# A two-model transformer kernel: a weight split moved behind the fifth step of the pair attention, early softmax inverses, and ScalarE's selection rows of the second mixer spread over four chunks

## What is computed

```python
def first_block(x, c, ctx, ...):                  # x and ctx: 256 tokens each
    for l in range(2):
        hx, hc = modulate(rms_norm(x, ...)), modulate(rms_norm(ctx, ...))
        qa, ka, va, qb, kb, vb, qc, kc, vc = split(hx @ w_in[l])      # and the same of hc
        oa = softmax attention, 8 heads;  ob = neighbourhood attention, 4 heads
        oc = diff_attend: (softmax(q0 k0) - lam * softmax(q1 k1)) v, 4 heads, then rms_norm
        x = x + gt1_x * (concat(oa, ob, oc) @ w_out[l])
        x = x + gt2_x * conv_ffn(...)             # in layer 0 the same for ctx
def second_block(x, meta_tokens, ...):            # 16 meta tokens + 256 tokens
    for l in range(2):
        h = h + 0.5 * rmsnorm(swiglu(...));  h = h + rmsnorm(token_mixer(...));  h = h + 0.5 * rmsnorm(swiglu(...))
def token_mixer(h, ...):
    fq, fk, fv, ff, gq, gk, gv, ga, gr, g_merge_a, g_merge_b = split(h @ w_in)
    log_f = log_sigmoid(ff + b_f)
    o_fox = fox_attention(fq, fk, fv, log_f)      # s + cum[q] - cum[k], softmax, 8 heads
    o_gla = gla_chunked(gq, gk, gv, log_a)        # exp of differences of cumulated log_a
    return (sigmoid(g_merge_a) * (o_fox @ w_fox_o) + sigmoid(g_merge_b) * (o_gla @ w_gla_o)) @ w_out
```

## Time and profile before

| | us |
|---|---|
| median of 3 runs | 2352.1 |
| lowest and highest | 2344.34 and 2356.29 |
| the profiled execution, device time | 2353.69 |
| its span, first to last instruction | 2351.9 |
| PE busy / DVE / ACT / POOL | 2301.4 / 1561.0 / 1207.0 / 145.0 |
| mean granted TensorE clock, of full | 0.988 |

### The profile page before, as it was taken

One profiled execution on the slowest core, in us unless ns is written; L12 is line 12 of the kernel. 1 busy time (PEld: TensorE's weight loads), 2 busy tenths in 40 slices (PEclk: granted clock), 3 DMA queues, 4 the chain that ended last, 5 costly groups with the idle time before them and its releaser, 6 DMA issues.

```text
span 2351.9 us, 46522 instructions
## 1 busy us (share of the span) xinstructions
PE 2301.4 (98%) x17227; PEld 2102.8 (89%) x17227; DVE 1561.0 (66%) x2770; ACT 1207.0 (51%) x2061; POOL 145.0 (6%) x252
## 2 busy tenths in 40 slices
PE   7999999999999999999999999999999999999998
PEld 5787788888878789999999889999999999899998
DVE  5546678887877458865655745766566557467764
ACT  4647544443237556654445555554454455656553
POOL 1214200000010220000000000000000000000000
PEclk9999999999999899999999999999999999999999
DMA  8750234444645025565555434455545553354654
GB/s 321 242 176 1 66 106 161 146 144 147 197 137 159 32 69 166 181 181 166 181 174 156 126 99 144 144 182 173 172 150 181 171 161 127 99 167 148 204 179 126
DMA packets 101199, 356.42 MB, mean 152 GB/s; under 512 B 11344, under 2 KB 13040, under 8 KB 101072
## 3 DMA queue, kind: packets, MB, share of 16 engines
q1 hardware_dynamic: 86704, 304.45, 40.5%
q0 software_dynamic: 14368, 50.24, 6.6%
HBM read 352.55 MB, written 1.05 MB: 150 GB/s over the span
## 4 chain that ended last, share of the span: by engine, by line
PE 92%; ACT 3%; DVE 3%; issue 1%; DMA 1%; SPq 0%; DVEq 0%; ACTq 0%
PE ps L782 25%; PE ps L784 25%; PE ps L783 25%; PE ps L957 2%; PE ps L973 2%; PE ps L940 2%; PE ps L799 2%; PE ps L803 1%; PE ps L800 1%; DMA ada_raw<-in_w_ada 1%; PE ps L1224 1%; PE ps L870 1%; ACT wh L1358 1%; PE ps L1266 1%; DVE wl L1848 1%
## 5 line engine op out<-in xcount | busy, mean ns | idle before, releaser
L1848 DVE TENSOR_TENSOR wl<-raw,wh 128x1024 fp32r<-128x1024 f32 x574 | 701.5, 1223 | 403.0 <-ACT wh L1358 402.4
L782 PE MATMUL ps<-hH,wh 128*128 128x272 f32 (+2 forms) x2880 | 888.5, 309 | 4.0 <-DVE silu L2548 3.1
L783 PE MATMUL ps<-hL,wh 128*128 128x272 f32 (+2 forms) x2880 | 876.7, 304 | 0.0
L784 PE MATMUL ps<-hH,wl 128*128 128x272 f32 (+2 forms) x2880 | 876.7, 304 | 0.0
L1358 ACT ACTIVATE wh<-raw 128x1024 fp32r<-128x1024 f32 x574 | 602.6, 1052 | 323.4 <-PE ps L784 305.5
L782 PEld LDWEIGHTS ps<-hH,wh 128*128 128x128 f32 x2880 | 545.4, 189 | 33.4 <-issue 4.3
L783 PEld LDWEIGHTS ps<-hL,wh 128*128 128x128 f32 x2880 | 545.3, 189 | 20.4 <-issue 0.2
L784 PEld LDWEIGHTS ps<-hH,wl 128*128 128x128 f32 x2880 | 545.5, 189 | 19.9
L784 PE MATMUL ps<-actH,wl 128*128 128x272 f32 (+2 forms) x1184 | 358.5, 303 | 0.0
L782 PE MATMUL ps<-actH,wh 128*128 128x272 f32 (+2 forms) x1184 | 356.4, 301 | 0.2 <-ACT actH L1518 0.2
L783 PE MATMUL ps<-actL,wh 128*128 128x272 f32 (+2 forms) x1184 | 356.4, 301 | 0.0
(11 more groups left out here) (308 smaller groups left out, 2803.4 us busy)
## 6 DMA issues: line engine op xcount, KB each, us to landing
raw<-in_w_ffn_gu SPq DMA_DIRECT2D x176, 512.0 KB, 3.5
raw<-in_w_mix SPq DMA_DIRECT2D x98, 512.0 KB, 3.5
raw<-in_w_up SPq DMA_DIRECT2D x88, 512.0 KB, 3.5
raw<-in_w_ffn_down SPq DMA_DIRECT2D x64, 512.0 KB, 3.6
ada_rest<-in_w_ada POOLq DMA_DIRECT2D x32, 512.0 KB, 4.8
raw<-in_w_out SPq DMA_DIRECT2D x32, 512.0 KB, 3.5
raw<-in_w_down SPq DMA_DIRECT2D x32, 512.0 KB, 3.5
raw<-in_w_qk SPq DMA_DIRECT2D x26, 512.0 KB, 5.2
```

What stands on the lines that cost most here:

```text
L782: pe.matmul(out, a_h, b_h, start=start, stop=False)
L783: pe.matmul(out, a_h, b_l, start=False, stop=False)
L784: return pe.matmul(out, a_l, b_h, start=False, stop=stop)
L1848: dve.tensor_tensor(wl[:, slot, :], raw[:, slot, :], wh[:, slot, :].bitcast(F32), ALU.subtract).then_inc(l_split, 1)
```

## The change

It has five parts.

1. In the pair attention the transposes of steps 0 and 1 come one position earlier: a new function `turned_at(i)` gives step 0 at i = 2, step 1 at i = 3, none at i = 4, and i-3 from i = 5 on. PE, ACT's copies and DVE's copies follow it.
2. The reciprocals of steps 0 and 1 move out of the loop, to right behind the exponentials of each, beside the values' projection (new function `inverse`).
3. ACT does the exponentials of step 1 ahead of its last copy to `v_tok`, and DVE the copy L2434 ahead of the last `rest_rows` and without a split in front of it.
4. The fifth split of stage `v{l}` (chunk 2 of `out{l}`), ACT's half and DVE's half, moves from the end of the values' stage to the end of i = 5 of the attention's loop. The table load L1436 goes.
5. In the mixers the four `nsel` instructions move from `ci` = 8, where they stood ahead of the edges' exponentials, to `ci` = 11, 12, 13 and 14, one each, behind the exponential of that chunk's level. The wait of the forgetting attention's first scores counts 4 per layer instead of 1.

```diff
+        def turned_at(i):
+
+            return i - 2 if i in (2, 3) else i - 3 if i >= 5 else None
...
@@ PE, pair_attention
-                    if 3 <= i < n + 3:
-                        turn(run[i - 3])
+                    if turned_at(i) is not None and turned_at(i) < n:
+                        turn(run[turned_at(i)])
@@ PE, scores of the forgetting attention
-                        pe.wait_ge(mix_set, l + 1)
+                        pe.wait_ge(mix_set, 4 * (l + 1))
@@ ACT, pair_attention
-                act.preload_act_table_set("natural_log_exp_and_others")
...
-                    if 3 <= i < n + 3:
-                        copy_even(run[i - 3])
+                    if turned_at(i) is not None and turned_at(i) < n:
+                        copy_even(run[turned_at(i)])
...
+                    if i == 5:
+                        split(S[f"v{l}"], Step(0, 4, RING))
@@ ACT, values_to_sbuf
-                    for i in range(w):
+                    late = which == 2
+                    for i in range(w - late):
                         split(st, Step(0, j + i, RING))
+                    if late:
+                        after(which)
...
-                    after(which)
+                    if not late:
+                        after(which)
@@ ACT, mix
-                    if ci == Z_AT + 4:
-
-                        act.wait_ge(pool_set, 7 * (l + 1))
-                        for r in (0, 32, 64, 96):
-                            last = act.activation(nsel[r:r + 8], ident[r:r + 8, r:r + 8].unsqueeze(2).to_broadcast([8, 8, P]),
-                                                  ACT.Copy, scale=-1.0)
-                        last.then_inc(mix_set, 1)
...
+                    if EDGE_AT + 2 <= ci < EDGE_AT + 6:
+                        if ci == EDGE_AT + 2:
+                            act.wait_ge(pool_set, 7 * (l + 1))
+                        r = 32 * (ci - EDGE_AT - 2)
+                        act.activation(nsel[r:r + 8], ident[r:r + 8, r:r + 8].unsqueeze(2).to_broadcast([8, 8, P]),
+                                       ACT.Copy, scale=-1.0).then_inc(mix_set, 1)
@@ DVE
+            def inverse(st):
+
+                dve.wait_ge(pair_exp, st.g + 1)
+                sums = slice(0, 2 * st.tiles)
+                dve.reciprocal(hinv[:, st.g % 4, sums], hsum[:, st.g % 4, sums]).then_inc(pair_inv, 1)
...
-                    if 1 <= i < n + 1:
-                        st = run[i - 1]
-                        dve.wait_ge(pair_exp, st.g + 1)
-                        sums = slice(0, 2 * st.tiles)
-                        dve.reciprocal(hinv[:, st.g % 4, sums], hsum[:, st.g % 4, sums]).then_inc(pair_inv, 1)
-                    if 3 <= i < n + 3:
-                        st = run[i - 3]
+                    if 1 <= i < n + 1 and not run[i - 1].early:
+                        inverse(run[i - 1])
+                    if turned_at(i) is not None and turned_at(i) < n:
+                        st = run[turned_at(i)]
...
+                    if i == 5:
+                        split(S[f"v{l}"], Step(0, 4, RING))
@@ DVE, ahead of the attention
-                for first in pair_steps(l)[:2]:
-                    largest(first)
+                first, second = pair_steps(l)[:2]
+                largest(first)
+                inverse(first)
+                largest(second)
                 split(st, Step(0, 3, RING))
-                rest_rows(15)
-                split(st, Step(0, 4, RING))
+                inverse(second)
                 bank = (st.g0 + 4) % 4
                 dve.wait_ge(chunk_used, RING + st.n0 + 5)
                 dve.tensor_copy(v_tok[:, 2:4, 3 * P:5 * P],
                                 ps[:, bank, :].rearrange("p (t c) -> p t c", c=2 * P)).then_inc(bank_free[bank], 1)
+                rest_rows(15)
```

## The result

The changed kernel takes **2335.0 us** (median of 8 executions, 2332.5 to 2337.3) against 2349.8 us for the kernel before (8 executions beside it, 2344.3 to 2356.3). The ratio is 0.9938 with a 95% interval of 0.9927 to 0.9948: faster by 0.62%. The forecast was 2338.0 with a range of 2328 to 2347 and "faster by over 0.5%" as the likeliest case.

A forecast was written before the change was run, and what follows sets the result against it. PE was busy for 2301 of 2352 us, so only its waits and half-clock stretches counted. Gains of 6.3 + 7.1 + 2.2 = 15.6 us off 2353.7 gave 2338.1, forecast as 2338, range 2328 to 2347.

The forecast's parts named there:

- Gain up to i = 6: Pair attention, layer 0, projection's end to scores of step 6: 17.1 us shrinks to 9.0 at full clock, gain 8.1 us.
- New wait: Attention, layer 0: the split moved to i = 5 delays DVE's copy for transposes 4; PE waits 1.8 us once.
- Net: Attention, layer 0: gain of 8.1 less the wait of 1.8 leaves 6.3 us.
- The lower bound: Layer 0's wait behind the moved split would be 0 if ACT ran far enough ahead.
- Attention, layer 1: Pair attention, layer 1: gain 8.3 us less a wait of 1.15 behind the moved split, net 7.1.
- Mixers, waits: Both mixers: PE's wait of 1.10 us ahead of `cross` goes, 2.2 us together; moved `nsel` instructions cost nothing.
- Mixers, clock: Behind `cross`: small matmuls, not only the wait, bring the clock down, so the fall stays; gain 0.
- Rival (b): Behind `cross` the clock stays up: 3.4 us per mixer, 2335 for one, 2331 for both; chance 0.21.
- Rival (a): Attention: the new wait brings the clock down; 2344 in one layer (chance 0.23), 2350 in both (0.08).
- The base: Starting time of the sum: the profiled execution of the kernel before, 2353.7 us.
- The sum: Whole kernel: 6.3 and 7.1 from the attention's layers plus 2.2 from the mixers, 15.6 us gained.

The follow-up runs named there:

- e3: Changed kernel with ACT's half of the moved split put right behind ACT's last copy to `v_tok`, DVE's half left at the end of i = 5; 2330.6 us.
- e8: Changed kernel with each of the four `nsel` instructions done four times over; 2347.2 us.
- e11: e6 with the twelve matmuls of `cross` done twice over in each mixer; 2342.9 us.
- e1: Changed kernel with the four `nsel` instructions back ahead of the edges' exponentials, so only the attention's parts 1 to 4; 2341.3 us.
- e10: Changed kernel with ACT's table load put back ahead of the attention's loop; 2333.7 us.
- e2: Kernel before with only the `nsel` instructions spread over four chunks (part 5 alone); 2344.4 us.
- e7: Changed kernel with the transposes of steps 0 and 1 back at i = 3 and 4; 2337.0 us.
- e12: e2 without the four filler matmuls ahead of `cross`; 2343.5 us.
- e9: Kernel before with eight filler matmuls ahead of `cross` instead of four; 2346.4 us.
- e6: e3 without the four filler matmuls ahead of `cross`; 2328.0 us.
- e4: Changed kernel with the fifth split back in front of the copies to `v_tok`, on ACT and DVE; 2343.6 us.

## Why the prediction was right, and where it was not

- **Attention, layer 0.** Gain up to i = 6 said 8.1: the stretch was to take 9.0 us and took 9.0. New wait said 1.8, measured 1.75. Net said 6.3, measured 6.3. The chain by which the wait was worked out (four exponentials, ACT's half, DVE's half, maximum, copy) is the one in the timelines, and e3 confirms its cause. DVE did not let the maximum of step 6 pass the split that waited: it stood idle for 2.49 us and did the maximum behind it. The lower bound, a wait of 0 if ACT ran far enough ahead, is what e3 reached. The 17.1 us before also hold 0.66 us in which PE waited for POOL's scaling of step 0, which the prediction did not name as a wait; POOL began it at 169.84 before and at 162.53 in the changed kernel, where the reciprocal comes early.
- **Attention, layer 1.** Said 7.1 net with a wait of 1.15; measured 6.9 with 1.27.
- **Mixers, waits.** Said 2.2, and both went. The four single rows cost nothing, as said; the reason given (2.9 us idle, 1.06 fits) is confirmed by e8, which finds where it ends.
- **Mixers, clock: the step that failed.** The prediction took it that the small matmuls and not only the wait bring the clock down, and so that the fall stays, gain 0. It was worth 6.85 - 2.2 = 4.65 us in the profile. The observation was true (e11), the conclusion was not: how long the clock stays down depends on all that is thin together, and the 1.10 us of waiting were part of it. Rival (b) had this mechanism. That its 2335 for one mixer is also the median is partly luck, as it stands on the same base, which was 4 us too high.
- **Rival (a).** It got 0.31 and is not refuted by the result: the profile of the changed kernel shows no fall behind the new wait, e1 and e8 with the same attention do, in 3 of 4 places (over all profiles with a wait of this size 3 of 9). Its price was mis-sized. I took 6 us per layer from the stretch of 13.6 us; the falls seen there were 6.8, 3.4 and 6.8 us long, 1.7 to 3.4 us each.
- **The base, and the attention's clock as a mean.** The sum went from one profile whose clock of 0.988 was low for this kernel: 74 further executions average 0.9913. The prediction's 15.6 are 2.59 + 2.26 + 2.2 - 1.8 - 1.15 = 4.1 of named waits and 11.5 of clock and handovers. PE's idle time fell by 5.1, the 4.1 and the 0.66 for POOL among them, so the waits were right. If they are the same in every execution, the other 9.7 of the 14.8 us are clock; by mean clocks it would be 20.4 us lost before less 11.4 after, 9.0, an estimate that agrees but is rough, since e10 by the same measure should be 4.4 us faster than the changed kernel and is 1.3 faster. So the clock, read from one execution, was where the sum failed: by the medians the attention gave 8.4 (e1) to 9.4 (after against e2) where the sum says 13.4, and the mixers 5.3 (e2) to 6.3 (after against e1) where it says 2.2. The base was 4 us above the median as well (2353.7 against 2349.8); the three errors (base, clock of the attention, clock of the mixers) partly cancel, and that 2338 lies so near 2335 is in part luck.
- **What was not in it:** 2.4 us at the program's start. The half clock there differs from execution to execution and stands ahead of everything that the change touches: 17.1 us in the profiles of after, e7 and e12, 10.2 in that of before, none in those of e1, e9 and e10.

## What to carry to other kernels

A split or any two-engine step moved out of a stall belongs, half by half, where each engine idles: here ACT's half behind the exponentials (four in layer 0, two in layer 1) cost 3.0 us of PE's waits, and in ACT's idle time, in e3, none. Price a wait of the matrix engine ahead of thin work (half-height scores, small blocks) at more than its length, but take what the clock costs from the times of many executions, since one profile shows only one outcome. Fillers made of small matmuls should be tried against nothing at all once the wait that they covered is gone.

## What was not expected of the hardware

- The granted clock fell with PE busy throughout: 3.3 us after the start of 24 small matmuls it went to 0.50 for 10.2 us (e11).
- A stretch at half clock can cost next to nothing: with 10.2 us of it at the program's start the projection of layer 0 ends at 166.9 to 168.0 us (before, e2, e3, e6, e8), without it at 166.7 to 167.1 (e1, e9, e10).
- Filler matmuls of 128 columns did not hold the clock: with 1.95 us of them in place of 0.98 us and most of the 1.10 us wait, it fell for 6.8 and 3.4 us (e9).
- The same code gave different stretches: behind the same wait of 1.75 us 0, 6.8, 6.8 and 0 us (after, e1, e8, e10). In e4 the runs spread from 2337 to 2351 us with clocks of 0.996 to 0.987.
